# First weights and first piece of x loaded in f32 by the hardware queues and rounded on the chip, in a hybrid decoder layer

## What is computed

```python
proj = x @ w_in                      # q | k | v | attention gate | conv h, B, C, gate | merge logits
# mixer B: three head groups (window, dilation) = (128,1), (512,4), (2048,16)
#          softmax over the window, groups combined by their softmax denominators
y_att  = (att * silu(g_att)) @ w_att_out
# mixer A: short gated causal convolution of three taps
y_conv = (b_c * conv3(c_c * h_c) * silu(g_conv)) @ w_conv_out
merged = sigmoid(gl_c + b) * y_conv + sigmoid(gl_a + b) * y_att
out    = layer_norm(2**0.25 * x + merged @ w_o)
```

## Time and profile before

| | us |
|---|---|
| median of 3 runs | 935.04 |
| lowest, highest | 935.03, 936.23 |
| the profiled execution | 934.47 |
| its span, slowest core (core 7) | 932.9 |
| spans of the 8 cores | 931.8 to 932.9 |

### The profile page before, as it was taken

The page is one execution under the profiler, slowest core; times in us unless marked ns, Lnnn a source line. Parts: engine busy times, 40 slices in busy tenths (PEclk is TensorE's granted clock), DMA queues, the critical chain, the costliest instruction groups (busy, mean ns, idle before and its releaser), DMA issues.

```text
span 932.9 us, 15665 instructions; the slowest of 8 cores (931.8 to 932.9 us)
## 1 busy us (share of the span) xinstructions
PE 901.7 (97%) x5904; PEld 500.9 (54%) x5904; DVE 465.8 (50%) x685; ACT 373.7 (40%) x546; POOL 74.2 (8%) x86
## 2 busy tenths in 40 slices
PE   3999999999999999999999999999999999999994
PEld 2796865558585875455544444444444444444441
DVE  3233455745365544755675455554733333333686
ACT  0103258742555226857562222222322222222575
POOL 5000000000000000000000000000000000000265
PEclk9999999999999999999999999999999999999998
DMA  9996112111200212111222212212295111200474
GB/s 129 159 166 90 24 24 34 24 24 24 46 13 1 47 24 35 24 24 28 42 46 46 43 27 45 44 20 40 40 208 151 35 32 31 37 1 0 129 267 169
DMA packets 21674, 55.83 MB, mean 60 GB/s; under 512 B 1760, under 2 KB 9952, under 8 KB 21216
## 3 DMA queue, kind: packets, MB, share of 16 engines
q0 software_dynamic: 16560, 36.97, 24.7%
q1 hardware_dynamic: 4896, 17.59, 5.4%
q10 hardware_dynamic: 144, 0.26, 0.1%
HBM read 83.39 MB, written 8.39 MB: 98 GB/s over the span
## 4 chain that ended last, share of the span: by engine, by line
PE 93%; DMA 2%; issue 1%; DVE 1%; ACT 1%; POOL 0%; DVEq 0%; ACTq 0%; POOLq 0%; SPq 0%
PE pp L433 86%; PE pp L660 4%; PE pp L632 3%; DMA wr<-ws 2%; ACT PT L638 0%; DMA out<-ob 0%; ACT Uacc L688 0%; POOL ob L896 0%; DVE Uacc L681 0%; DVE aT L696 0%; POOL xO L397 0%; DVE rz L692 0%; DVE PT L647 0%; ACT rz L690 0%; DVE ys L837 0%
## 5 line engine op out<-in xcount | busy, mean ns | idle before, releaser
L433 PE MATMUL pp<-xO,wr 128*128 128x512 bf16 x2432 | 539.1, 379 | 1.5 <-DMA wr<-ws 1.3
L433 PEld LDWEIGHTS pp<-xO,wr 128*128 128x128 bf16 x2432 | 234.6, 98 | 282.2 <-issue 5.7
L638 ACT ACTIVATE PT<-pp 128x1024 bf16<-128x1024 f32 x96 | 93.1, 1022 | 95.2 <-PE pp L632 87.5
L433 PE MATMUL pp<-wr,xO 128*128 128x256 bf16 x768 | 87.9, 275 | 12.9 <-DMA xO<-xo 12.9
L478 DVE CAST V<-pp 128x512 bf16<-128x512 f32 (+1 forms) x74 | 48.3, 655 | 88.2 <-PE pp L433 88.1
L433 PEld LDWEIGHTS pp<-wr,xO 128*128 128x128 bf16 x768 | 81.1, 119 | 18.7 <-issue 13.2
L344 POOL DMA_DIRECT2D wr<-ws x54 | 28.8, 535 | 753.3 <-PE pp L433 596.5
L811 DVE TENSOR_TENSOR mS<-pp,gcS 128x512 f32<-128x512 f32 x32 | 22.1, 691 | 116.1 <-PE pp L433 116.1
L681 DVE TENSOR_TENSOR Uacc<-Uacc,pp 128x512 f32<-128x512 f32 x64 | 52.8, 869 | 51.9 <-PE pp L660 51.6
L647 DVE TENSOR_TENSOR PT<-PT,mk_bf 128x1024 bf16<-128x1024 bf16 x96 | 65.4, 690 | 25.8 <-ACT PT L638 23.7
L498 ACT ACTIVATE KT<-pp 128x512 bf16<-128x512 f32 x72 | 41.5, 583 | 76.6 <-PE pp L433 76.4
(11 more groups left out here) (59 smaller groups left out, 666.6 us busy)
## 6 DMA issues: line engine op xcount, KB each, us to landing
wr<-ws POOLq DMA_DIRECT2D x42, 512.0 KB, 6.3
xt<-xtok SPq DMA_DIRECT2D x16, 512.0 KB, 6.6
out<-ob SPq DMA_DIRECT2D x15, 512.0 KB, 3.5
xH<-xh POOLq DMA_DIRECT2D x4, 1024.0 KB, 56.0
wr<-ws POOLq DMA_DIRECT2D x8, 384.0 KB, 6.1
xO<-xo POOLq DMA_DIRECT2D x4, 512.0 KB, 16.8
xO<-xo POOLq DMA_DIRECT2D x2, 1024.0 KB, 32.4
wo<-wo POOLq DMA_DIRECT2D x2, 1024.0 KB, 20.3
```

What stands on the lines that cost most here:

```text
L433: inst = e.matmul(ps[bank][:, c0:c0 + n], lhs[k], rhs[k], start=(k == 0), stop=(k == len(lhs) - 1))
L638: S.add("act", lambda e: e.activation(out=PT[h][:, :], in_=pp[h][:, :], func=AF.Exp), writes=[("PT", h)], banks=[2 * h, 2 * h + 1])
```

## The change

Weight unit 0 and piece 0 of x no longer come through POOL's converting DMAs. They are loaded in f32 into buffers that lie over `Uacc` and `gatt` (not yet in use): `wst` by SP, `xs` in two halves by ACT. ACT and DVE each round a half of the weights and a half of each half of x to bf16. POOL's next load, and so all that it issues, waits until the first half of `xs` has landed. The ones of group 1 and 0 are filled ahead of the rounding, those of group 2 after piece 1.

```diff
+        xs = at("xs", o_ua, [128, 8, 512], F32)
+        wst = at("wst", o_ua + 16384, [128, UW], F32)
+        S.over(n_U, [("xs", h) for h in range(2)])
+        S.over([("gatt", m) for m in range(4)], ["wst"])
...
-        def load_next():
+        def load_next(behind=()):
...
-                  writes=[("wr", i)], dma=f"wr{i}")
+                  reads=behind, writes=[("wr", i)], dma=f"wr{i}")
...
-            S.parts[("xO", w)] = [("xOa", w), ("xOb", w)]
+            S.parts[("xO", w)] = [("xOa", w), ("xOb", w)] + ([("xOc", 0), ("xOd", 0)] if w == 0 else [])
...
-        load_next()
-        load_x(True, 0, 0)
-        load_x(True, 0, 1)
-        load_next()
+        def ones_in(g):
+            ones = V[g][:, :].rearrange("p (b c) -> p b c", c=192)[:, :, 64:128]
+            S.add("dve", lambda e: e.memset(ones, 1.0), writes=[("Vone", g)])
+
+        ones_in(1)
+        ones_in(0)
+
+        u0 = order.pop(0)
+        slots[u0], left[u0] = free.pop(0), uses_of(u0)
+        S.add("sp", lambda e: [e.dma_start(out=wst[:], in_=ws_d[UIDX[u0]])], writes=["wst"], dma="wst")
+        for h in range(2):
+            S.add("act", lambda e, h=h: [e.dma_start(out=xs[:, 4 * h:4 * h + 4, :],
+                                                     in_=xo_d[0][:, 2048 * h:2048 * h + 2048].rearrange("p (k c) -> p k c", c=512))],
+                  writes=[("xs", h)], dma=f"xs{h}")
+        w0t, w0n = wr[slots[u0]], ("wr", slots[u0])
+        S.add("act", lambda e: e.activation(out=w0t[:, 0:1024], in_=wst[:, 0:1024], func=AF.Copy), reads=["wst"], writes=[w0n])
+        S.add("dve", lambda e: e.tensor_copy(out=w0t[:, 1024:2048], in_=wst[:, 1024:2048]), reads=["wst"], writes=[("wrb", slots[u0])])
+        S.parts[w0n] = [w0n, ("wrb", slots[u0])]
+        for h in range(2):
+            S.add("act", lambda e, h=h: e.activation(out=xO[:, 0, 4 * h:4 * h + 2, :], in_=xs[:, 4 * h:4 * h + 2, :], func=AF.Copy),
+                  reads=[("xs", h)], writes=[("xO" + "ab"[h], 0)])
+            S.add("dve", lambda e, h=h: e.tensor_copy(out=xO[:, 0, 4 * h + 2:4 * h + 4, :], in_=xs[:, 4 * h + 2:4 * h + 4, :]),
+                  reads=[("xs", h)], writes=[("xO" + "cd"[h], 0)])
+        load_next([("xs", 0)])
         load_next()
...
-        for g in (1, 0, 2):
-            ones = V[g][:, :].rearrange("p (b c) -> p b c", c=192)[:, :, 64:128]
-            S.add("dve", lambda e, ones=ones: e.memset(ones, 1.0), writes=[("Vone", g)])
...
-                        pieces = [(XPART[half], w) for _, w in pieces]
+                        pieces = [(XPART[half], w) for _, w in pieces] + [(XPART[2 + half], 0) for _, w in pieces if w == 0]
...
+            if w == 1:
+                ones_in(2)
```

More of the change, by code:

```diff
@@ L289, in build @@
         esems = {e: es.enter_context(nc.semaphore("sem_" + e)) for e in Sched.ENGS}
-        dsems = [es.enter_context(nc.semaphore(f"dsem{i}")) for i in range(32)]
+        dsems = [es.enter_context(nc.semaphore(f"dsem{i}")) for i in range(40)]
         S = Sched(nc, esems, dsems)
-        n_xO = [("xOa", 0), ("xOb", 0), ("xOa", 1), ("xOb", 1), ("xO", 2), ("xO", 3)]
+        n_xO = [("xOa", 0), ("xOb", 0), ("xOc", 0), ("xOd", 0), ("xOa", 1), ("xOb", 1), ("xO", 2), ("xO", 3)]
         n_xH = [("xH", w) for w in range(4)]
@@ L435, in proj @@
             S.add("pe", fn, reads=list(reads), banks=[bank])
-        ALLK, XH, XPART = range(8), (range(0, 4), range(4, 8)), ("xOa", "xOb")
+        ALLK, XH, XPART = range(8), (range(0, 4), range(4, 8)), ("xOa", "xOb", "xOc", "xOd")
         class Proj:
```

## The result

The changed kernel is slower: 941.86 us median (941.59 to 942.21 in 5 runs) against 935.04 us, ratio 1.0071 with a 95% interval from 1.0055 to 1.0087. The forecast was 934.1 us, in a range from 932.3 to 936.6 us. In some executions of these kernels the cores of one or both dies run at a lower granted clock and the time is 4 to 20% longer; the ratios leave these out, the medians in microseconds do not.

The account below looks back on a forecast made before the run. TensorE bounds the kernel, and only its start can give time back: D moves from 22.88 to 21.95 us, -0.9 us, so the median goes from 935.04 to 934.1 us. The range was 932.3 to 936.6 us.

Parts of the forecast that it names:

- D: Run of forty-eight matmuls after C; forecast to start at 21.95 us instead of 22.88 us, with 910.0 us after it.
- Step 1: Hardware loads at the start: f32 weights and first half of x, 2.1 MB at 0.37 MB/us, landed at 8.6 us.
- T: Landing time of the f32 weights and first half of x: 8.6 us, with ends of 8.0 and 9.7 us.
- A: TensorE's first sixteen matmuls of 256 columns; forecast to start at 12.2 us.
- Step 2: Rounding by ACT and DVE, with ACT's table load of 1.28 us: A starts at T + 3.5 us.
- Step 3: TensorE's first matmuls: A and B take 6.3 us, C 3.45 us, so D starts at 21.95 us.
- B: TensorE's second sixteen matmuls of 256 columns; forecast to follow A without a wait.
- C: Sixteen matmuls of 512 columns, K and Q of piece 0; possible at 18.5 us, taking 3.45 us.
- Step 4: POOL's software stream: its first two landings at 15.8 and 20.0 us, both hidden, by 2.7 and 1.95 us.
- Step 5: DVE's fills of ones: the third, 3.47 us, moves behind the casts of piece 1, about 36 us; cost nothing.
- the slower one: Rival, 938.2 us: software stream starves the second half of x, landed at T + 11.0 us; D at 26.1 us; chance 0.14.
- The wash: Rival, 935.1 us: hardware loads no faster than the cast stream, T at 9.7 us, D at 22.95 us; chance 0.20.

Follow-up runs that it names:

- one queue: The changed kernel with all f32 loads on SP's queue: weights, first half of x, second half, then constants; 936.16 us, 1.0013 times the kernel before.
- the early release: The one queue kernel with POOL's loads released by the weights, not by the first half of x; 936.03 us, 1.0013 times the kernel before.

## Why the prediction was wrong

The account on the slowest core: D at 29.84 us, forecast 21.95 us, 7.9 us apart.

1. **Step 1, the landing T, failed.** It said the weights and the first half of x land together at 8.6 to 8.7 us, with an upper end of 9.7 us. The first half did land at about 8.5 us. The weights landed at 16.46 us, which is 7.8 of the 7.9 us. Two errors are in it.
 - I counted only the 2.1 MB that A needs, as if the second half of x, issued at once by the same engine, would stand behind both. It stands behind the first half alone, on its own queue, and shares with the weights; and the weights, issued 0.4 us later, began only when three quarters of the first half were through (0.78 MB by 6.5 us). Giving the weights the same start brought them to 12.2 us at worst. That is about 4 us.
 - The rate, and the end of the load. I took 0.37 MB/us, and 1.8 us for the fixed part. From 2 to 12 us the changed kernel moved 0.245 MB/us, the two better orders 0.263 and 0.268 (the last two windows below). With the weights first, 2.1 MB at 0.263 are 8.0 us where I had 5.7. The other 1.2 us of the landing at 12.2 us come at the end: the queues had taken up the last of the bytes by 10.4 us. That is the remaining 3.5 us. The row of 406 GB/s, from one core with little company, did not hold here, and my lower bound, from the steady cast stream, was too high for the first microseconds. Why they are slower no run shows.

Cores 1 and 3 of the kernels with the weights first and with one queue:

```profile
2.00:12.00 10.00, 0.00 (x0) 0.00 (x0) 3.74 (x2) 0.00 (x0) 0.00 (x0) 1.00 0.97 263
```

```profile
2.00:12.00 10.00, 0.00 (x0) 0.00 (x0) 4.80 (x4) 2.72 (x3) 0.00 (x0) 1.00 0.96 268
```

2. **Step 2 was right.** From landing to A 3.55 us, forecast 3.5; the table load 1.28 us and its ACTIVATE right behind it, 1.06 and 0.99 us for the casts. The Trainium skill (ScalarE: Activation LUTs, What ACT_TABLE_LOAD costs) puts a drain of about 1.38 us beside the load; the estimate with it was 4.9 us, and the trace has no such gap. DVE was hidden, its casts 0.88 us and 1.0 us each.

3. **Step 3 was right**: A and B 6.38 us on the slowest core (6.3), C 3.45 us, and 910.5 us after D (910.0). B did not wait.

4. **Step 4 was too cheap, which did not show.** POOL's first load took 9.5 us to land, not 6.9, since the f32 loads still had the engines. It was hidden because A was so late. With one queue it took 8.0 us, A starts at 12.93 us and C waits 2.44 us for it.

5. **Step 5 was right**: the third fill of ones begins at 45.54 us and no wait of TensorE follows from it.

Of the rivals, the slower one had a hardware load starved by company, but the wrong victim and the wrong company. The wash had the right reason, the f32 loads no faster than the casts, and lacked the order. None stated that two loads needed together, on two queues, with a third behind one of them, do not land together.

What the change could have gained is answered in part: with the weights first and the table load early it is 1.0010. One queue together with the early table load was not run. Before, the start waited for source bytes to be read (240 GB/s), and the f32 loads read the same bytes at nearly the same rate (245 GB/s); the rounding then comes on top, on the path.

## What to carry to other kernels

Add up all that is in flight when a load is needed, not only what is needed, and put loads that one instruction needs together on one queue in the order of need, with the rest behind: here A then began at 12.93 us, not at 15.78 us, and the next loads became the wait. In this start, with the DMA engines over 0.9 busy, hardware queues read no faster than the casting one (245 to 268 GB/s against 240 GB/s); what they added was the rounding. The first ACTIVATE of this program brought its 1.28 us table load to wherever it stood, and a one-element ACTIVATE during the first loads took it off the path, for 1.30 us.

## What the runs showed that I had not expected

A head start of 0.43 us between two queues became 4 us of landing: from 4 to 6 us one queue moved 0.42 MB and the other nothing, and equal shares came only later.

A wait between A and B could keep TensorE at the lower pace. In the kernel with the early release A ran at it for 3.57 or 3.58 us on cores 1, 3, 5 and 7, and after waits of 1.03 to 1.39 us B took 3.57 or 3.58 us too. On cores 0, 2, 4 and 6, where A took 3.30 to 3.58 us and the waits were 0.67 to 1.41 us, B took 1.91 us (0.21 and 0.11 us a matmul, the paces of 1.2 and 2.4 GHz; the granted-clock column has 1.00 for both). What decides it no run shows. In the kernel before, a wait of 1.28 us ahead of C, behind a B at the higher pace, cost nothing of the kind.
